# A two-layer hybrid decoder trunk: the high halves of the weights by a converting DMA, and silu through tanh

## The chip, the cores and the metric

One NeuronCore of a Trainium2 chip runs the whole program. The metric is the device time of that core in microseconds (us); lower is better.

## What is computed

Two layers, each `x + W_out[concat(mixer_g(h) * silu(z_g))]` with `h = RMSNorm(x)`, on 512 tokens of width 2048 in float32. One input projection (2048 to 7192 columns) feeds four groups of four heads. Cut to what matters:

```
h = rms_norm(x, norm_g)
p = einsum('btd,dp->btp', h, w_in)
ya = gla_mixer(aq, ak, av, alr, ...)  * silu(az)      # gated linear attention
yb = swa_mixer(bq, bk, bv, ...)       * silu(bz)      # sliding window with sinks
yc = diff_mixer(cq, ck, cv, ...)      * silu(cz)      # differential attention
yd = gdn_mixer(dqkv, dbeta, da, ...)  * silu(dz)      # gated DeltaNet
y  = concatenate([ya, yb, yc, yd]);   x = x + einsum('btm,md->btd', y, w_out)
# inside gdn_mixer:  qkv = silu(causal_conv(qkv, conv_w))
```

`silu(v) = v * sigmoid(v) = v / (1 + exp(-v))`.

## The kernel before

**Products in split precision.** Every float32 operand of a projection is split into a high half, its value rounded to `fp32r`, and a low half, the remainder. A product is three matmuls: high by high, high by low, low by high. The activations' halves (`actT_hi`, `actT_lo`) are made by ScalarE and VectorE once a layer; the weights' halves are made while they stream.

**The weight stream.** The weights lie in HBM as blocks of 128x512; one block is the weight side of one k-tile. Two blocks in a row are a pair, 128 rows of 4 KB, 512 KB. A layer has 288 k-tiles or 144 pairs, the whole program 288 pairs. SyncE (SP) brings pair `i` to `w_raw` (four buffers) once `raw_used` says that its buffer is free. GpSimd (POOL) makes from each k-tile the high half `w_hi` (line 376: add zero, write as `fp32r`) and the low half `w_lo` (line 380: `w_raw - w_hi`); both are rings of four k-tiles. It waits at line 375 for `kt_done`, so that the ring's place is free: k-tile `n` is begun when TensorE has finished k-tile `n - 4`. TensorE waits at line 407 for `w_ready`, which counts finished low halves, and then does 12 matmuls of 512 columns (line 421): three terms for each of four accumulators `acc`.

**The order of the work** is written out by hand, per engine; engines meet only through semaphores. In `project` TensorE takes a column chunk of the projection, 16 k-tiles long (12 or 4 in the output projection). Between its k-tiles it takes steps of a mixer, a generator (`gdn`, `gla`, `swa`, `dif`) whose steps are spread evenly over the chunk. A mixer's step waits in TensorE's queue for what VectorE (DVE) or ScalarE (ACT) made of the step before; while it waits, the projection behind it stands too. A layer goes through these stages:

- the chunks dq, dk, dv, dz, without a mixer (64 k-tiles). VectorE evicts dq, dk and dv (`turned_out`, line 1232) and runs the convolution and its silu over them (`conv`, lines 1252 to 1265), in the order: evict dq, convolve dq, evict dk, convolve dk, evict dv, convolve dv. TensorE cannot start the chunk after dk or dv before the accumulators are evicted
- four chunks with `gdn` for 128 tokens each, four with `gla`, two with `swa` (two token tiles each): 160 k-tiles
- four chunks of the output projection (12 k-tiles each) with `dif`, then four of 4 k-tiles each without a mixer.

**Silu.** ScalarE writes `exp(-z)` into a scratch tile (lines 916, 980, 1009, 1056, 1115). VectorE adds 1, takes the reciprocal and multiplies: lines 1260, 1263, 1265 for the 12 convolution blocks of a layer, and `gate`, lines 1197, 1199, 1201, for the 16 gates of a layer (4 mixers, 4 token tiles). In `swa` VectorE's queue reads: scores, maxima, sums for the next token tile, `gate`, the denominator, `normalise` of the next token tile (lines 1424, 1425, 1429), then the copy PT1 (line 1461) for which TensorE's product at line 660 waits. `normalise` itself waits for two inverse roots from ScalarE (line 1041; each is a Ln and an Exp with a table load ahead of both).

Of the kernel before, what the change touches and what calls it, by code (L numbers as in the profile page):

```python
# [39 lines left out]
RAW, RING = 4, 4  # L40
# [42 lines left out]
def names(fmt, *ranges):  # L83
    out = [""]
    for r in ranges:
# [25 lines left out]
    "g1 g2 g3 os redo y0 y1 y2 y3".split()  # L111


def hybrid_trunk(nc, x, wstream, wsmall, pcol, prow, wlr, cf, masks, out):
    ctx = ExitStack()
    with ctx:
# [11 lines left out]
        w_hi = sb("w_hi", [P, RING, GW], F32R)  # L128
# [105 lines left out]
        raw_used, hi_done, w_ready = sem("raw_used"), sem("hi_done"), sem("w_ready")  # L234
# [40 lines left out]
        S_DVE = Steps(sem("setup_dve"), ["ss"] + [f"rd{t}" for t in T] + ["smT", "b1", "beta", "nbeta", "av", "sp",  # L275
# [27 lines left out]
        def _(sp):  # L303
# [1308 lines left out]
```

## Time and profile before

| | us |
|---|---|
| median of 3 runs | 2127.36 (2125.7 to 2127.44) |
| the profiled execution | 2127.9 |
| its span in the trace | 2126.1 |
| TensorE busy | 2038.3 |
| GpSimd busy | 1396.3 |
| VectorE busy | 1026.4 |
| ScalarE busy | 537.6 |

The profiled execution is one run of the same program; 1.8 us of it lie outside the span. Matmuls overlap in the pipeline and their ends are modelled, so TensorE's busy time is no measure of its pace: the pace is read from how long a chain of matmuls takes, and what it loses from its waits. The granted clock is 1.00 at 2.4 GHz and 0.5 at 1.2 GHz; a stage's mean below 1.00 tells how much of it ran at the lower level.

### The profile page before, as it was taken

How to read it: one execution, taken by the hardware profiler on the slowest of the kernel's cores; microseconds unless marked ns; L12 is line 12 of the kernel's file. 1: busy time of each engine (PE TensorE's matmuls, PEld its weight loads, DVE VectorE, ACT ScalarE, POOL GpSimd, SP SyncE). 2: the span in 40 equal slices, each digit the busy share in tenths (PEclk: the TensorE clock that was granted, in tenths of full speed). 3: DMA queues.
4: the chain of work that ended last, by engine and by line, in shares of the span. 5: the costliest groups of instructions: out<-in, count | busy, mean ns of one | idle time of the engine just before them, and what ended most of it. 6: DMA issues, size and time to landing. Idle time of an engine off the chain costs nothing.

```text
span 2126.1 us, 25561 instructions
## 1 busy us (share of the span) xinstructions
PE 2038.3 (96%) x10300; PEld 1660.6 (78%) x10300; DVE 1026.4 (48%) x1407; ACT 537.6 (25%) x1014; POOL 1396.3 (66%) x1164
## 2 busy tenths in 40 slices
PE   7998999999999989999999999999999999999999
PEld 6877878878888878767888778778778787776777
DVE  1699453453222455565427984435432225545563
ACT  4010221222222443332320112221222225423220
POOL 6797654555777756557787975545557777555676
PEclk9999999999999999999999999999999999999999
DMA  5232211211222211422442322111122222132223
GB/s 216 74 96 80 70 60 50 60 60 60 80 81 88 80 60 63 146 69 80 129 132 72 99 79 63 57 60 59 51 62 87 80 80 84 55 127 81 74 85 119
DMA packets 50709, 175.92 MB, mean 83 GB/s; under 512 B 5566, under 2 KB 6304, under 8 KB 49568
## 3 DMA queue, kind: packets, MB, share of 16 engines
q1 hardware_dynamic: 44288, 155.75, 23.3%
q10 hardware_dynamic: 6304, 18.55, 2.3%
q8 instruction: 81, 1.33, 0.3%
q14 instruction: 36, 0.29, 0.0%
HBM read 165.89 MB, written 8.39 MB: 82 GB/s over the span
## 4 chain that ended last, share of the span: by engine, by line
PE 72%; DVE 20%; ACT 5%; issue 2%; DMA 1%; SPq 0%; ACTq 0%
PE acc L421 55%; DVE slots L1256 3%; DVE slots L1199 3%; DVE general L1263 3%; PE mix L488 2%; PE mix L499 1%; PE mix L682 1%; PE mix L660 1%; PE mix L528 1%; PE mix L491 1%; DVE slots L1252 1%; ACT slots L849 1%; DVE general L1319 1%; DVE slots L1429 1%; PE mix L774 1%
## 5 line engine op out<-in xcount | busy, mean ns | idle before, releaser
L376 POOL TENSOR_TENSOR w_hi<-w_raw,zeros 128x512 fp32r<-128x512 f32 x576 | 626.2, 1087 | 671.5 <-PE acc L421 648.2
L421 PE MATMUL acc<-w_hi,actT_hi 128*128 128x512 f32 x1920 | 789.0, 411 | 14.0 <-DVE slots L1232 12.1
L380 POOL TENSOR_TENSOR w_lo<-w_raw,w_hi 128x512 fp32r<-128x512 f32 x576 | 767.6, 1333 | 45.1
L421 PE MATMUL acc<-w_hi,actT_lo 128*128 128x512 f32 x1920 | 755.3, 393 | 0.0
L421 PE MATMUL acc<-w_lo,actT_hi 128*128 128x512 f32 x1920 | 753.5, 392 | 0.0
L421 PEld LDWEIGHTS acc<-w_hi,actT_hi 128*128 128x128 f32 x1920 | 364.9, 190 | 106.6 <-issue 38.7
L421 PEld LDWEIGHTS acc<-w_hi,actT_lo 128*128 128x128 f32 x1920 | 363.2, 189 | 80.3
L421 PEld LDWEIGHTS acc<-w_lo,actT_hi 128*128 128x128 f32 x1920 | 365.3, 190 | 65.5
L421 PE MATMUL acc<-actT_hi,w_hi 128*128 128x512 f32 x384 | 153.2, 399 | 2.9 <-DVE slots L1232 2.9
L421 PE MATMUL acc<-actT_hi,w_lo 128*128 128x512 f32 x384 | 150.4, 392 | 0.0
L421 PE MATMUL acc<-actT_lo,w_hi 128*128 128x512 f32 x384 | 150.4, 392 | 0.0
L849 ACT ACTIVATE slots<-acc,xr 128x512 f32<-128x512 f32 x88 | 60.2, 689 | 267.8 <-PE acc L421 267.7
L1199 DVE RECIPROCAL slots<-slots 128x512 f32<-128x512 f32 x32 | 107.3, 3353 | 1.1
L1256 DVE SCALAR_TENSOR_TENSOR slots<-slots,pcol_all 128x511 f32<-128x511 f32 (+2 forms) x72 | 99.1, 1376 | 2.6
L421 PEld LDWEIGHTS acc<-actT_hi,w_hi 128*128 128x128 f32 x384 | 72.7, 189 | 18.8 <-issue 2.2
L421 PEld LDWEIGHTS acc<-actT_hi,w_lo 128*128 128x128 f32 x384 | 72.6, 189 | 15.5
L421 PEld LDWEIGHTS acc<-actT_lo,w_hi 128*128 128x128 f32 x384 | 72.7, 189 | 15.0 <-issue 0.5
L1263 DVE RECIPROCAL general<-general 128x512 f32<-128x512 f32 x24 | 80.5, 3353 | 0.8
L916 ACT ACTIVATE general<-slots 128x512 f32<-128x512 f32 x24 | 15.2, 632 | 252.8 <-DVE slots L1256 252.8
L974 ACT ACTIVATE slots<-mix 128x512 f32<-128x512 f32 x40 | 24.0, 599 | 216.1 <-PE mix L488 216.1
L1480 DVE TENSOR_TENSOR slots<-acc,slots 128x512 f32<-128x512 f32 x64 | 42.7, 688 | 67.4 <-PE acc L421 67.4
L1376 DVE SCALAR_TENSOR_TENSOR slots<-mix,slots 128x256 f32<-128x256 f32 x8 | 3.4, 424 | 139.7 <-ACT slots L999 139.7
(250 smaller groups left out, 2095.5 us busy)
## 6 DMA issues: line engine op xcount, KB each, us to landing
w_raw<-in_wstream SPq DMA_DIRECT2D x288, 512.0 KB, 3.5
out_x<-slots ACTq DMA_DIRECT2D x7, 1024.0 KB, 4.4
slots<-in_x SPq DMA_DIRECT2D x4, 1024.0 KB, 14.5
slots<-in_x ACTq DMA_DIRECT2D x1, 4096.0 KB, 14.2
slots<-out_x ACTq DMA_DIRECT2D x1, 4096.0 KB, 15.0
out_x<-slots ACTq DMA_DIRECT2D x4, 256.0 KB, 2.3
cf_sb<-in_cf ACTq DMA_DIRECT2D x1, 964.0 KB, 11.4
slots<-in_masks ACTq DMA_DIRECT2D x1, 384.0 KB, 12.2
```

The costliest lines, as they stand in the source:

```text
L376: pool.tensor_tensor(w_hi[:, r], w_raw[:, s, k], zeros[:, :].broadcast_to([P, GW]), ALU.add) \
L380: pool.tensor_tensor(w_lo[:, r], w_raw[:, s, k], w_hi[:, r].bitcast(F32), ALU.subtract).then_inc(w_ready, 1)
L421: last = nc.tensor.matmul(acc[b][:, :], lhsT, rhs, start=(k == 0 and i == 0), stop=(k == kts - 1 and i == 2))
L488: last = nc.tensor.matmul(mh[3][:, h], U["MT"][:, h], U["X"][:, h], start=True, stop=True)
L491: last = nc.tensor.transpose(mh[1][:, h], U["X"][:, h], ident)
L499: last = nc.tensor.matmul(mh[0][:, h], U["XT"][:, h], U["Y"][:, h], start=True, stop=True)
L849: nc.scalar.activation(slot(SLOT[c])[:, b], acc[b][:, :], ACT.Copy, scale=xr[:, l, b:b + 1]) \
L974: nc.scalar.activation(U["Y"], mh[3], ACT.Copy).then_inc(*s(f"y{lv}"))
L1199: dve.reciprocal(tmp, tmp).then_inc(St.sem, St.one(f"{t}.g2"))
L1256: dve.scalar_tensor_tensor(dst[:, d:], src[:, 0:SEQ - d], tap[i], dst[:, d:], ALU.mult, ALU.add).then_inc(*ci(f"t{i}"))
L1263: dve.reciprocal(general[:, b % 2], general[:, b % 2]).then_inc(*ci("rec"))
L1480: dve.tensor_tensor(xs, acc[b][:, :], xs, ALU.add).then_inc(acc_free, 1)
```

## The change

Two parts. First, `w_hi` is no longer made by a GpSimd instruction. GpSimd issues for each pair a DMA from HBM straight into `w_hi`, now three buffers of a pair, whose type `fp32r` differs from the source's `float32`, so that the transfer converts. The source is the same `wstream` that SyncE still brings to `w_raw` (now three buffers); each weight is thus read twice. The DMA for pair `g + 1` is issued between the two low halves of pair `g`. Second, silu goes by `v * sigmoid(v) = (v/2) * (1 + tanh(v/2))`: `v` is halved where it is made (the gates' eviction scale `xr_half`, the convolution's taps), ScalarE does Tanh in place of Exp, and VectorE does one instruction in place of three.

```diff
-RAW, RING = 4, 4
+RAW, HI, RING = 3, 3, 4
...
-        w_hi = sb("w_hi", [P, RING, GW], F32R)
+        w_hi = sb("w_hi", [P, HI, 2, GW], F32R)
...
             def weights(i):
-                sp.wait_ge(raw_used, i + 1)
+                if i >= RAW:
+                    sp.wait_ge(w_ready, 2 * (i - RAW) + 2)
                 sp.dma_start(w_raw[:, i % RAW].rearrange("p a n -> p (a n)"),
...
+            def high_halves(g):
+
+                if g >= HI:
+                    pool.wait_ge(kt_done, RING + 2 * (g - HI) + 2)
+                pool.dma_start(w_hi[:, g % HI].rearrange("p a n -> p (a n)"),
+                               wstream[g:g + 1].rearrange("a p n -> p (a n)")).then_inc(hi_in[g % HI], 16)
+
+            high_halves(0)
...
-                    pool.wait_ge(raw_in[s], (l * (PAIRS // RAW) + i // RAW) * 16 + 16)
+                    pool.wait_ge(raw_in[g % RAW], g // RAW * 16 + 16)
+                    pool.wait_ge(hi_in[g % HI], g // HI * 16 + 16)
                     for k in range(2):
-                        n, r = 2 * i + k, (2 * i + k) % RING
-
-                        pool.wait_ge(kt_done, l * LAYER_KTS + (n + 1))
-                        pool.tensor_tensor(w_hi[:, r], w_raw[:, s, k], zeros[:, :].broadcast_to([P, GW]), ALU.add) \
-                            .then_inc(hi_done, 1)
-
-                        pool.wait_ge(hi_done, l * LAYER_KTS + (n + 1))
-                        pool.tensor_tensor(w_lo[:, r], w_raw[:, s, k], w_hi[:, r].bitcast(F32),
+                        n = 2 * g + k
+
+                        pool.wait_ge(kt_done, n + 1)
+                        pool.tensor_tensor(w_lo[:, n % RING], w_raw[:, g % RAW, k], w_hi[:, g % HI, k].bitcast(F32),
                                            ALU.subtract).then_inc(w_ready, 1)
-
-                    pool.wait_ge(w_ready, l * LAYER_KTS + (2 * i + 2))
-                    pool.sem_inc(raw_used, 1)
+                        if k == 0 and g + 1 < DEPTH * PAIRS:
+                            high_halves(g + 1)
...
+                    r = (xr_half if c in GATES else xr)[:, l, b:b + 1]
...
-                        nc.scalar.activation(general[:, b % 2], slot(CONV[c])[:, b], ACT.Exp, scale=-1.0) \
+                        nc.scalar.activation(general[:, b % 2], slot(CONV[c])[:, b], ACT.Tanh) \
...
+                taps = pcol_all[:, :, PC["conv"]:]
+                dve.tensor_scalar(taps, taps, 0.5, None, ALU.mult).then_inc(lam_steps, 1)
...
-                dve.tensor_scalar(tmp, tmp, 1.0, None, ALU.add).then_inc(St.sem, St.one(f"{t}.g1"))
-                dve.wait_ge(St.sem, St.at(l, f"{t}.g1"))
-                dve.reciprocal(tmp, tmp).then_inc(St.sem, St.one(f"{t}.g2"))
-                dve.wait_ge(St.sem, St.at(l, f"{t}.g2"))
-                dve.tensor_tensor(Zs, Zs, tmp, ALU.mult).then_inc(St.sem, St.one(f"{t}.g3"))
+                dve.scalar_tensor_tensor(Zs, tmp, 1.0, Zs, ALU.add, ALU.mult).then_inc(St.sem, St.one(f"{t}.g3"))
...
+                dve.tensor_scalar(xr_half[:, l], xr[:, l], 0.5, None, ALU.mult).then_inc(*si("half"))
...
-                        dve.tensor_scalar(general[:, b % 2], general[:, b % 2], 1.0, None, ALU.add) \
-                            .then_inc(*ci("one"))
-                        cw("one")
-                        dve.reciprocal(general[:, b % 2], general[:, b % 2]).then_inc(*ci("rec"))
-                        cw("rec")
-                        dve.tensor_tensor(dst, dst, general[:, b % 2], ALU.mult).then_inc(*ci("mul"))
+                        dve.scalar_tensor_tensor(dst, general[:, b % 2], 1.0, dst, ALU.add, ALU.mult) \
+                            .then_inc(*ci("mul"))
```

The four other gates' Exp become Tanh in the same way. The number of ScalarE's table loads is the same in both programs.

GpSimd's queue in the first layer's second chunk, two pairs long, before (the bracket holds the semaphores waited for; `raw_in2` is the landing of the pair's `w_raw`):

```order
L376 TENSOR_TENSOR w_hi<-w_raw,zeros 128x512 [waits kt_done,raw_in2]
L380 TENSOR_TENSOR w_lo<-w_raw,w_hi 128x512 [waits hi_done]
L376 TENSOR_TENSOR w_hi<-w_raw,zeros 128x512 [waits kt_done]
L380 TENSOR_TENSOR w_lo<-w_raw,w_hi 128x512 [waits hi_done]
L376 TENSOR_TENSOR w_hi<-w_raw,zeros 128x512 [waits w_ready,kt_done,raw_in3]
L380 TENSOR_TENSOR w_lo<-w_raw,w_hi 128x512 [waits hi_done]
L376 TENSOR_TENSOR w_hi<-w_raw,zeros 128x512 [waits kt_done]
L380 TENSOR_TENSOR w_lo<-w_raw,w_hi 128x512 [waits hi_done]
```

and the same engine and place now (`hi_in0` is the landing of the pair's converting DMA):

```order
L387 TENSOR_TENSOR w_lo<-w_raw,w_hi 128x512 [waits kt_done,hi_in0,raw_in0]
L369 DMA w_hi<-in_wstream 128x1024 [waits kt_done]
L387 TENSOR_TENSOR w_lo<-w_raw,w_hi 128x512 [waits kt_done]
L387 TENSOR_TENSOR w_lo<-w_raw,w_hi 128x512 [waits kt_done,hi_in1,raw_in1]
L369 DMA w_hi<-in_wstream 128x1024 [waits kt_done]
L387 TENSOR_TENSOR w_lo<-w_raw,w_hi 128x512 [waits kt_done]
```

The two instructions of a pair that made `w_hi` became one DMA issue, and the first `w_lo` of each pair has a new wait: the landing of a DMA that this queue issued one pair earlier.

VectorE's queue over one block of the convolution, before:

```order
L1252 TENSOR_SCALAR slots<-slots,pcol_all 128x512 [waits acc_free]
L1256 SCALAR_TENSOR_TENSOR slots<-slots,pcol_all 128x511 [waits conv_dve]
L1256 SCALAR_TENSOR_TENSOR slots<-slots,pcol_all 128x510 [waits conv_dve]
L1256 SCALAR_TENSOR_TENSOR slots<-slots,pcol_all 128x509 [waits conv_dve]
L1260 TENSOR_SCALAR general<-general 128x512 [waits conv_act]
L1263 RECIPROCAL general<-general 128x512 [waits conv_dve]
L1265 TENSOR_TENSOR slots<-slots,general 128x512 [waits conv_dve]
```

and now:

```order
L1257 TENSOR_SCALAR slots<-slots,pcol_all 128x512 [waits acc_free]
L1261 SCALAR_TENSOR_TENSOR slots<-slots,pcol_all 128x511 [waits conv_dve]
L1261 SCALAR_TENSOR_TENSOR slots<-slots,pcol_all 128x510 [waits conv_dve]
L1261 SCALAR_TENSOR_TENSOR slots<-slots,pcol_all 128x509 [waits conv_dve]
L1265 SCALAR_TENSOR_TENSOR slots<-general,slots 128x512 [waits conv_act]
```

The block ends in one instruction behind the same wait for ScalarE (`conv_act`), where it ended in three.

## Rows read from the trace of the kernel before

**Rows 1.** Waits, TensorE's own: line waited, releaser, us in total, times, longest.
```profile
PE mix L660 <- DVE slots L1461: 20.0, 6, 3.9
PE acc L421 <- DVE slots L1232: 15.0, 4, 6.1
PE mix L682 <- DVE slots L1495: 8.9, 2, 4.5
PE mix L528 <- DVE general L1352: 6.6, 8, 0.8
```

**Rows 2.** Stretches: start:end, us, busy us of PE, PEld, DVE, ACT, POOL; PEclk, DMA share, GB/s.
```profile
74.00:183.50 109.50, 101.85 (x443) 83.37 (x442) 97.39 (x79) 9.41 (x17) 86.59 (x67) 0.97 0.27 82
...
527.00:731.00 204.00, 204.00 (x1028) 163.52 (x1027) 47.72 (x75) 54.68 (x93) 148.81 (x128) 1.00 0.27 83
731.00:827.00 96.00, 85.47 (x406) 71.50 (x405) 56.91 (x76) 46.83 (x92) 55.70 (x46) 0.93 0.20 61
...
1071.00:1235.00 164.00, 156.66 (x691) 128.35 (x691) 109.88 (x99) 22.48 (x44) 132.73 (x107) 0.98 0.30 92
```

**Rows 3.** The chain of waits in order of time: start, us, 16 k-tiles of 12 matmuls.
```profile
183.52 43.66 PE acc L421 x192
```

**Rows 4.** Groups by line, VectorE, silu: count, busy us, mean ns, idle before.
```profile
L1199 DVE RECIPROCAL slots<-slots 128x512 f32<-128x512 f32 x32 | 107.3, 3353 | 1.1
...
L1263 DVE RECIPROCAL general<-general 128x512 f32<-128x512 f32 x24 | 80.5, 3353 | 0.8
...
L1201 DVE TENSOR_TENSOR slots<-slots 128x512 f32<-128x512 f32 x32 | 39.8, 1244 | 1.1
...
L1265 DVE TENSOR_TENSOR slots<-slots,general 128x512 f32<-128x512 f32 x24 | 20.2, 840 | 0.8
...
L1197 DVE TENSOR_SCALAR slots<-slots 128x512 f32<-128x512 f32 x32 | 17.1, 535 | 20.8 <-ACT slots L980 20.8
...
L1260 DVE TENSOR_SCALAR general<-general 128x512 f32<-128x512 f32 x24 | 14.0, 582 | 16.8 <-ACT general L916 16.8
```

**Rows 5.** Timeline of VectorE in `swa`, first token tile: start, us, instruction, count.
```profile
745.89 1.63 DVE L1201 TENSOR_TENSOR slots<-slots 128x512 f32<-128x512 f32 x1
...
750.59 3.19 DVE L1429 TENSOR_TENSOR slots<-slots,stat 128x512 f32<-128x512 f32 x2
753.71 0.41 DVE L1461 COPY slots<-mix 128x256 f32<-128x256 f32 x1
```

**Rows 6.** Timeline of ScalarE there: the two inverse roots' last instructions.
```profile
745.80 0.21 ACT L1041 ACTIVATE stat<-stat 128x6 f32<-128x6 f32 x1
...
748.95 0.22 ACT L1041 ACTIVATE stat<-stat 128x16 f32<-128x16 f32 x1
```

**Rows 7.** Timeline of VectorE in the third token tile of `swa`.
```profile
811.80 2.13 DVE L1429 TENSOR_TENSOR slots<-slots,stat 128x512 f32<-128x512 f32 x2
```

**Rows 8.** Timeline of ScalarE there.
```profile
810.89 0.22 ACT L1041 ACTIVATE stat<-stat 128x16 f32<-128x16 f32 x1
```

**Rows 9.** Timeline of VectorE in `dif`: four evictions behind the gate.
```profile
900.37 0.69 DVE L1201 TENSOR_TENSOR slots<-slots 128x512 f32<-128x512 f32 x1
900.98 2.48 DVE L1480 TENSOR_TENSOR slots<-acc,slots 128x512 f32<-128x512 f32 x4
```

**Rows 10.** The page's groups of GpSimd: count, busy us, mean ns, idle before.
```profile
L376 POOL TENSOR_TENSOR w_hi<-w_raw,zeros 128x512 fp32r<-128x512 f32 x576 | 626.2, 1087 | 671.5 <-PE acc L421 648.2
...
L380 POOL TENSOR_TENSOR w_lo<-w_raw,w_hi 128x512 fp32r<-128x512 f32 x576 | 767.6, 1333 | 45.1
```

**Rows 11.** The page's DMA queue of SyncE, and issues: KB each, median us to landing.
```profile
q1 hardware_dynamic: 44288, 155.75, 23.3%
...
w_raw<-in_wstream SPq DMA_DIRECT2D x288, 512.0 KB, 3.5
out_x<-slots ACTq DMA_DIRECT2D x7, 1024.0 KB, 4.4
```

**Rows 12.** Timeline of TensorE at the start.
```profile
17.75 1.09 PE L729 MATMUL mix<-cf_sb,slots 128*128 128x128 f32 x4 [3.68 <-DMA slots<-in_x]
```

More of the change, by code:

```diff
@@ L95 @@
 GDN_DVE = ("ag red qn kn qd kb ke ei es0 es1 es2 es3 mt qk xi x1 xt2 x2 xt3 x3 xt4 x4 xt5 x5 xt6 xt7 "
-           "g1 g2 g3 ub v00 v01 v02 v03 s00 s01 s02 s03 v10 v11 v12 v13 s10 s11 s12 s13 redo y0 y1 y2 y3").split()
+           "g3 ub v00 v01 v02 v03 s00 s01 s02 s03 v10 v11 v12 v13 s10 s11 s12 s13 redo y0 y1 y2 y3").split()
 GLA_PE = "u cum dec tr a us o".split()
 GLA_ACT = "abs e l eb enb er dect qkT gate sqo0 sqo1 lno ro".split()
-GLA_DVE = "g qd ki ke at0 at1 s00 s01 s10 s11 g1 g2 g3 redo y0 y1 y2 y3".split()
+GLA_DVE = "g qd ki ke at0 at1 s00 s01 s10 s11 g3 redo y0 y1 y2 y3".split()
 SWA_PE = "tr s0 s1 pt0 pt1 pv".split()
 SWA_ACT = "gate qT kT p0 p1 p2 p3 es PT0".split()
-SWA_DVE = "b0 b1 b2 b3 mx mxs nm es g1 g2 g3 den rd PT1 y0 y1 y2 y3".split()
+SWA_DVE = "b0 b1 b2 b3 mx mxs nm es g3 den rd PT1 y0 y1 y2 y3".split()
 PREP_PE = "q k".split()
@@ L150, in hybrid_trunk @@
         xr = sb("xr", [P, DEPTH, TILES])
+        xr_half = sb("xr_half", [P, DEPTH, TILES])
         def slot(n):
@@ L233, in hybrid_trunk @@
         dve_passed, pe_passed = sem("dve_passed"), sem("pe_passed")
-        raw_used, hi_done, w_ready = sem("raw_used"), sem("hi_done"), sem("w_ready")
+        hi_in = [sem(f"hi_in{i}") for i in range(HI)]
+        w_ready = sem("w_ready")
         ws_hi_done, ws_ready = sem("ws_hi_done"), sem("ws_ready")
@@ L274, in hybrid_trunk @@
                       [f"yhi{k}" for k in range(KT)])
-        S_DVE = Steps(sem("setup_dve"), ["ss"] + [f"rd{t}" for t in T] + ["smT", "b1", "beta", "nbeta", "av", "sp",
+        S_DVE = Steps(sem("setup_dve"), ["ss", "half"] + [f"rd{t}" for t in T] + ["smT", "b1", "beta", "nbeta", "av", "sp",
                                                                     "glog", "gA", "zero_gdn"] +
@@ L278, in hybrid_trunk @@
         CONV_DVE = Steps(sem("conv_dve"), [f"{c}{b}{s}" for c in ("dq", "dk", "dv") for b in range(4)
-                                           for s in ("t3", "t2", "t1", "t0", "one", "rec", "mul")])
+                                           for s in ("t3", "t2", "t1", "t0", "mul")])
         CONV_ACT = Steps(sem("conv_act"), [f"{c}{b}" for c in ("dq", "dk", "dv") for b in range(4)])
@@ L322, in _ @@
             x_in(3)
-            weights(3)
             for l in range(DEPTH):
@@ L404, in project @@
                         ahead(k)
-                    r = (kt0 + k) % RING
+                    n = l * LAYER_KTS + kt0 + k
+                    hi, lo = w_hi[:, n // 2 % HI, n % 2], w_lo[:, n % RING]
                     pe.wait_ge(w_ready, l * LAYER_KTS + (kt0 + k + 1))
@@ L414, in project @@
                         if turned:
-                            terms = [(w_hi[:, r, c], actT_hi[:, a]), (w_hi[:, r, c], actT_lo[:, a]),
-                                     (w_lo[:, r, c], actT_hi[:, a])]
-                        else:
-                            terms = [(actT_hi[:, a, c], w_hi[:, r]), (actT_hi[:, a, c], w_lo[:, r]),
-                                     (actT_lo[:, a, c], w_hi[:, r])]
+                            terms = [(hi[:, c], actT_hi[:, a]), (hi[:, c], actT_lo[:, a]), (lo[:, c], actT_hi[:, a])]
+                        else:
+                            terms = [(actT_hi[:, a, c], hi), (actT_hi[:, a, c], lo), (actT_lo[:, a, c], hi)]
                         for i, (lhsT, rhs) in enumerate(terms):
@@ L979, in _ @@
                         act.wait_ge(acc_free, acc_free_after(l, CHUNKS.index("dz"), 3))
-                    nc.scalar.activation(U["GATE"], gz, ACT.Exp, scale=-1.0).then_inc(*s("gate"))
+                    nc.scalar.activation(U["GATE"], gz, ACT.Tanh).then_inc(*s("gate"))
                     take_out(l, CHUNKS[4 + t])
@@ L1008, in _ @@
                     gz = slot(SLOT["az"])[:, t].rearrange("p (h c) -> p h c", h=HEADS)
-                    nc.scalar.activation(V["GATE"], gz, ACT.Exp, scale=-1.0).then_inc(*s("gate"))
+                    nc.scalar.activation(V["GATE"], gz, ACT.Tanh).then_inc(*s("gate"))
                     w(A_PE, "o")
@@ L1056, in _ @@
                     nc.scalar.activation(W["GATE"], slot(SLOT["bz"])[:, t].rearrange("p (h c) -> p h c", h=HEADS),
-                                         ACT.Exp, scale=-1.0).then_inc(*s("gate"))
+                                         ACT.Tanh).then_inc(*s("gate"))
                     w(B_PE, "tr")
@@ L1115, in _ @@
                     nc.scalar.activation(Z["GATE"], slot(SLOT["cz"])[:, t].rearrange("p (h c) -> p h c", h=HEADS),
-                                         ACT.Exp, scale=-1.0).then_inc(*s("gate"))
+                                         ACT.Tanh).then_inc(*s("gate"))
                     for h in H:
```

10 lines of the change are left out of this document (5 added, 5 removed).

## The prediction

> **What bounds the kernel now.** I read the waits first. TensorE waits for others in few places, and nearly all of them name VectorE [rows 1]: the output step of `swa` for the copy PT1 (20.0 us in 6 waits), the projection for the evictions of dk and dv behind the convolution (15.0 in 4), a score step of `dif` (8.9 in 2), and a state step of `gdn` (6.6 in 8). The reader is to see that GpSimd is not in this list: it makes the weight halves in time. Next the stretches [rows 2]: where those waits are long, the mean granted clock is below 1.00, so the 1.2 GHz level follows them. A clock of 0.97 over 109.5 us costs 109.5 x 0.03 = 3.3 us, 0.98 over 164.0 us another 3.3, 0.93 over 96.0 us (once in each layer) 6.7. Last the pace: 16 k-tiles in a row took 43.66 us [rows 3], 2.73 per k-tile and 5.46 per pair. 576 k-tiles make 1572 us of matmuls that this change leaves alone; the mixers' own matmuls fill most of the rest. What can be won is waits and the clock behind them; what can be lost is a weight that comes later than every 5.46 us.
>
> **Silu on VectorE.** Three instructions cost 0.54 + 3.35 + 1.24 = 5.1 us for a gate and 0.58 + 3.35 + 0.84 = 4.8 for a convolution block [rows 4]. The one that replaces them reads two SBUF tiles as L1201 and L1265 do, so I take their 0.84 to 1.24. Saved: 3.9 us for each of 32 gates, 3.5 to 4 for each of 24 blocks, some 210 us of VectorE's time. On the path only this counts:
>
> (a) Evictions of dk and dv. Four blocks stand ahead of the first and eight ahead of the second in each layer, at least 14 and 28 us sooner, where the longest wait is 6.1 [rows 1]. All 15.0 us go, and with them the slow clock, 3.3 + 3.3 [rows 2]: **21.6 us**. Next late there is TensorE itself.
>
> (b) `gdn`: 3.9 us sooner against a longest wait of 0.8 [rows 1]: **6.6 us**.
>
> (c) `swa`: here the gain is cut. VectorE's L1429 waits for ScalarE's second inverse root, which ends at 748.95 + 0.22 = 749.17; L1429 starts at 750.59 [rows 5, 6]. It can come 1.4 us sooner, not 3.9, and PT1 with it. In the third tile it starts at 811.80 and the root ends at 811.11 [rows 7, 8]: 0.7 us; the second I take as the third. Per layer 2.8, together 5.6 of the 20.0. What is late next is ScalarE with its table loads, which the change leaves. Of the 6.7 us per layer of slow clock I count a quarter: 1.7 x 2 = 3.4. Sum **9.0 us**.
>
> (d) `dif`: behind the gate stand four evictions, 2.48 us, that today start the moment the gate ends [rows 9]. With the gate 3.9 us shorter three of them (0.62 each, 1.9) can run before TensorE's chunk is over; the fourth cannot. I take 1.5 per layer, **3.0 us** of the 8.9.
>
> (e) The new halvings (twice 128x4 values, once the taps) have instructions of some 0.2 us and hide under the next transfer or chunk; Tanh takes Exp's place in the same count of instructions and table loads: 0.
>
> Sum of (a) to (e): 40.2 us.
>
> **The weights.** GpSimd loses 576 instructions of 1.09 us and keeps 576 of 1.33 [rows 10]. As it is waited for nowhere today, this gives TensorE nothing directly. VectorE shares something with it: L1201 took 1.24 us on average and the same operation in L1265 0.84 [rows 4]. Fewer such overlaps shorten steps before waits that stay; I take 2 us off, between 0 and 6.
>
> What it adds is 288 issues and a loop. The DMA of pair g+1 is issued after the first low half of pair g, and that low half waits for the landing of pair g. One turn is therefore L + 1.33 us, with L from issue to landing, and TensorE wants a pair every 5.46 us where no mixer slows it. So there is no cost up to **L = 4.1 us**. Above it the stock drains: when the issue is made on time, TensorE has four k-tiles, 10.9 us, before it needs the result, a slack of 10.9 - (L + 1.33). The pure run in each layer is dk, dv and dz, 24 pairs; `gla` goes at 204.0 / 32 = 6.38 us a pair [rows 2]. Price at L = 5.0: 2 x (24 x 0.87 - 4.6) = 33 us. At L = 5.5: 2 x (24 x 1.37 - 4.1) + 64 x 0.45 = 58 + 29 = 87 us.
>
> No row shows L for a converting DMA from GpSimd. Below: the same bytes from SyncE land in 3.5 us [rows 11]; lower would change nothing. Above: 1.09 us, the GpSimd instruction that it replaces, for the software's work, and 4.4, a transfer of twice the bytes, for running beside `w_raw`'s [rows 10, 11]: 5.5. That is no wall: a conversion that slows the movement would go beyond. I take L = 4.3, near the lower row, since it is the same transfer with an issue that is dearer, and `w_raw`'s own is issued only when the second low half is done, so they overlap little. Cost: 24 x 0.17 = 4.1 us per run, less than its slack of 5.3; I put down 1. The DMA engines hold it: `q1` moved 155.75 MB in 23.3% of the span, 314 GB/s, so a pair takes 1.7 us, two of them 3.3 of 5.46.
>
> The Trainium skill, "DMA: Bandwidth & Descriptors", section "Anatomy of one DMA — SWDGE (gpsimd) path", gives 2.0 us + bytes / 436 GB/s; for 512 KB that is 3.2 us, against the 3.5 of SyncE's row. By it the loop would take 4.5 us, the 1 us above would not be paid, and the sum would be 2087.
>
> At the start TensorE waits for the second slice of x until 17.75 us [rows 12]; the first high pair now goes among these transfers: +1.7 us.
>
> **Sum.** The profiled execution took 2127.9 (span 2126.1), 0.5 above the median of 2127.36. 2127.9 - 40.2 - 2 + 1 + 1.7 = 2088.4, as a median **2088 us**.
>
> **Rivals.**
> 1. *The loop becomes the bound.* TensorE then waits for `w_lo` in the pure chunks and, further up, in `gla`. It decides from L = 5.1, where its price reaches the 40 us. For it: a wait that did not exist, one DMA in flight at a time, unknown software and conversion. Against: 3.5 us in [rows 11], and DMA engines less than two thirds busy. At L = 5.5 the time is 2087 + 87 = 2174; at 6 it would be over 2240. Chance 0.28.
> 2. *The loop eats part*: L from 4.7 to 5.1, 2100 to 2128. Chance 0.09, a third of it within 0.2%.
> 3. *VectorE holds up the DMA's issue.* L1252 (tensor_scalar, SBUF to SBUF) runs in each convolution block and overlaps GpSimd's work, as L1201's swing above suggests for two-input ones. If one in five of the 64 pairs of the first chunks lost some 1.2 us (the 1.24 of L1201), that is 15 us: 2103. Chance 0.05. The Trainium skill, "SBUF — State Buffer", section "SBUF: two separate sides", warns of this: an fp32 VectorE operation that uses both ports keeps GpSimd from writing descriptors. No row here shows it, as no DMA starts from GpSimd.
> 4. *Only the convolution's waits go*, as every mixer step has another late partner: 2127.9 - 21.6 + 2 = 2108. Chance 0.03.
> 5. That the DMA copies and does not round would leave the time as it is forecast; it is inside the first case.
>
> **The numbers.** The forecast case has 0.55: 2068 (6 us from overlaps, and about half of what `swa` keeps of waits, 14 us, gone too) to 2100. 0.2% is 4.3 us, about what a measurement of this kernel can tell from no change. Faster by more: 0.55 + 0.05 + 0.03 + 0.04 = 0.67. Within: 0.04. Slower: 0.29. The range from 2068 to 2174 reaches to the upper bound of L and leaves out what lies beyond.
>
> **What would show it.** Right: no wait on L1237 (the evictions) in TensorE's list; PEclk 1.00 from 74 to 183 us; the wait of `swa`'s output step (line 660 before) still there, at some 14 us; the converting DMA's median landing from 3.9 to 4.5 us; no wait of TensorE for `w_lo`; k-tiles of 2.73 us in dk, dv and dz. Wrong: landings over 5 us, with TensorE waiting for GpSimd's `w_lo` and the pair pace of dv at L + 1.3. If landings are short and the time is still above 2100, then (c) or (a) failed: see which engine TensorE's waits name.

## The result, and the profile after

The changed kernel takes **2064.38 us** (median of 4 runs, 2062.99 to 2070.53) against 2126.53 for the kernel before in the same session: ratio 0.9714, 95% interval 0.9693 to 0.9735, 62 us faster. I had forecast 2088, with a range down to 2068. The direction was right, the size was not: the time lies 3.6 us below the low end.

The page of the changed kernel, busy times, the weight groups of GpSimd, and the DMA issues:

```profile
PE 2020.5 (98%) x10300; PEld 1651.3 (80%) x10300; DVE 722.4 (35%) x1298; ACT 536.4 (26%) x1014; POOL 921.9 (45%) x876
...
PE 89%; ACT 6%; DVE 3%; issue 1%; DMA 1%; SPq 0%; ACTq 0%; DVEq 0%
...
L387 POOL TENSOR_TENSOR w_lo<-w_raw,w_hi 128x512 fp32r<-128x512 f32 x576 | 756.1, 1313 | 750.4 <-DMA w_hi<-in_wstream 441.9
...
L369 POOL DMA_DIRECT2D w_hi<-in_wstream x288 | 163.6, 568 | 385.9 <-PE acc L426 377.0
...
w_hi<-in_wstream POOLq DMA_DIRECT2D x288, 512.0 KB, 3.9
w_raw<-in_wstream SPq DMA_DIRECT2D x288, 512.0 KB, 4.4
```

The second line is the chain that ended last, by engine: TensorE is 89% of it. The converting DMA lands after 3.9 us; `w_raw`, which had the DMA engines to itself before, now takes 4.4 [rows 11]. GpSimd waits 441.9 us for the high halves, and that harms nobody, as TensorE's own waits show (line waited, releaser, us in total, times, longest):

```profile
PE mix L734 <- DMA slots<-in_x: 13.9, 1, 13.9
PE mix L665 <- DVE slots L1462: 10.9, 6, 2.7
PE mix L687 <- DVE slots L1496: 7.3, 2, 3.7
PE mix L456 <- DVE slots L1304: 6.6, 6, 1.9
PE mix L477 <- ACT slots L977: 2.2, 8, 0.3
```

Against [rows 1]: the evictions (15.0) are gone, PT1 (now L665 <- L1462) fell from 20.0 to 10.9, `dif` (L687 <- L1496) from 8.9 to 7.3; the state step of `gdn` is gone; no wait names `w_lo`. L456 waits for the product ag of the next token tile of `gdn`. Before, this wait was the fourth in the list, and I used it nowhere:

```profile
PE mix L451 <- DVE slots L1303: 10.9, 6, 1.8
```

The same stretches as in [rows 2]:

```profile
74.00:183.50 109.50, 109.50 (x491) 90.62 (x490) 62.66 (x71) 10.68 (x19) 61.02 (x56) 1.00 0.61 177
527.00:731.00 204.00, 203.06 (x1026) 163.06 (x1018) 40.99 (x83) 64.98 (x113) 101.01 (x96) 1.00 0.56 165
731.00:827.00 96.00, 90.46 (x463) 76.32 (x464) 33.57 (x71) 40.69 (x82) 39.15 (x38) 0.98 0.46 137
1071.00:1235.00 164.00, 164.00 (x734) 135.30 (x733) 76.07 (x85) 16.82 (x29) 92.58 (x87) 1.00 0.61 179
```

TensorE has no gap in the first and the last of them, and the clock is 1.00 in both. VectorE's groups that answer to [rows 4]: line, shape, count, busy us, mean ns, idle before.

```profile
L1261 DVE SCALAR_TENSOR_TENSOR slots<-slots,pcol_all 128x511 f32<-128x511 f32 (+2 forms) x72 | 69.7, 968 | 2.6
L1265 DVE SCALAR_TENSOR_TENSOR slots<-general,slots 128x512 f32<-128x512 f32 x24 | 26.4, 1099 | 16.8 <-ACT general L922 16.8
L1205 DVE SCALAR_TENSOR_TENSOR slots<-slots 128x512 f32<-128x512 f32 x32 | 23.4, 732 | 20.8 <-ACT slots L986 20.8
```

The first is a surprise: the change does not touch the convolution's taps, and before they took

```profile
L1256 DVE SCALAR_TENSOR_TENSOR slots<-slots,pcol_all 128x511 f32<-128x511 f32 (+2 forms) x72 | 99.1, 1376 | 2.6
```

**Where the time came from.** I cut the traces where a k-tile's first matmul starts and sum both layers (us; a stage's length is the distance of these starts, and the last stage ends with the start of the last matmul). The columns for the two parts alone are from the first experiment. All four are profiled executions; that of the changed kernel was the longest of its four runs (2070.53), so its column shows 57.4 us less than before where the medians differ by 62.

| stage | before | silu alone | DMA alone | both (the change) | forecast gain, gain |
|---|---|---|---|---|---|
| dk, dv, dz and their evictions | 286.8 | 266.5 | 271.7 | 265.4 | 21.6, 21.4 |
| `gdn` | 595.9 | 589.5 | 578.2 | 579.2 | 6.6, 16.7 |
| `gla` | 410.4 | 410.4 | 410.4 | 410.4 | 0, 0 |
| `swa` | 259.9 | 244.4 | 240.4 | 243.1 | 9.0, 16.8 |
| output projection, `dif` | 437.6 | 436.9 | 439.7 | 436.0 | 3.0, 1.6 |
| start and both dq chunks | 131.7 | 130.7 | 130.8 | 130.7 | -1.7, 1.0 |

`gdn` carries the largest miss, 10.1 us, and `swa` the next, 7.8. The slow clock in these stages, the length of each stretch times what its granted clock lacked to 1.00, was 6.8, 0, 13.7 and 3.4 us before (first row, `gdn`, `swa`, output) and 0, 0, 5.1 and 6.8 in this profile; in `gdn` the clock has no part.

### The profile page after: what moved, and what is told of

Its sections match the earlier page's. It is cut to its first block, busy times and chain, and to the rows that moved or that the text cites. A ratio compares the mean times of both kernels' runs of the same rounds, so it can differ in the third digit from the quotient of the medians.

```text
span 2068.7 us, 24875 instructions
## 1 busy us (share of the span) xinstructions
PE 2020.5 (98%) x10300; PEld 1651.3 (80%) x10300; DVE 722.4 (35%) x1298; ACT 536.4 (26%) x1014; POOL 921.9 (45%) x876
## 4 chain that ended last, share of the span: by engine, by line
PE 89%; ACT 6%; DVE 3%; issue 1%; DMA 1%; SPq 0%; ACTq 0%; DVEq 0%
PE acc L426 70%; PE mix L493 2%; PE mix L504 1%; PE mix L687 1%; ACT L1047 1%; ACT L1044 1%; PE mix L706 1%; PE mix L496 1%; PE mix L533 1%; PE mix L665 1%; PE mix L526 1%; ACT slots L855 1%; PE mix L779 1%; PE mix L734 1%; PE mix L538 1%
## 5 line engine op out<-in xcount | busy, mean ns | idle before, releaser
L387 POOL TENSOR_TENSOR w_lo<-w_raw,w_hi 128x512 fp32r<-128x512 f32 x576 | 756.1, 1313 | 750.4 <-DMA w_hi<-in_wstream 441.9
L369 POOL DMA_DIRECT2D w_hi<-in_wstream x288 | 163.6, 568 | 385.9 <-PE acc L426 377.0
L855 ACT ACTIVATE slots<-acc,xr 128x512 f32<-128x512 f32 x56 | 38.3, 690 | 159.5 <-PE acc L426 159.4
L1261 DVE SCALAR_TENSOR_TENSOR slots<-slots,pcol_all 128x511 f32<-128x511 f32 (+2 forms) x72 | 69.7, 968 | 2.6
L1335 DVE COPY slots<-mix 128x512 f32<-128x512 f32 x40 | 27.7, 691 | 85.7 <-PE mix L496 85.7
L855 ACT ACTIVATE slots<-acc,xr_half 128x512 f32<-128x512 f32 x32 | 21.9, 689 | 125.8 <-PE acc L426 125.8
```

Of the source, the lines that this page charges most:

```text
L369: pool.dma_start(w_hi[:, g % HI].rearrange("p a n -> p (a n)"), wstream[g:g + 1].rearrange("a p n -> p (a n)")).then_inc(hi_in[g % HI], 16)
L387: pool.tensor_tensor(w_lo[:, n % RING], w_raw[:, g % RAW, k], w_hi[:, g % HI, k].bitcast(F32), ALU.subtract).then_inc(w_ready, 1)
L855: nc.scalar.activation(slot(SLOT[c])[:, b], acc[b][:, :], ACT.Copy, scale=r) \
L1261: dve.scalar_tensor_tensor(dst[:, d:], src[:, 0:SEQ - d], tap[i], dst[:, d:], ALU.mult, ALU.add).then_inc(*ci(f"t{i}"))
L1335: dve.tensor_copy(U["XT"], mh[1]).then_inc(*s(f"xt{lv}"))
```

## The experiments

**1. The two parts alone.** The silu part alone keeps this in GpSimd's loop, with the rings of before:

```diff
-                        if k == 0 and g + 1 < DEPTH * PAIRS:
-                            high_halves(g + 1)
...
+                        pool.tensor_tensor(w_hi[:, r], w_raw[:, s, k], zeros[:, :].broadcast_to([P, GW]), ALU.add) \
+                            .then_inc(hi_done, 1)
```

> The silu part of the change alone: x sigmoid(x) by the hyperbolic tangent, but GpSimd still makes the high halves with its own add, so it makes two passes of 1.1 and 1.3 us for every k-tile as before. Theory A: the changed kernel gained 10 us more in the gdn chunks than the sum had (16.7 against 6.6 us over two layers), because GpSimd lost half its passes and VectorE's operations with two SBUF operands no longer run beside them (the conv taps took 1376 ns before and 968 after, the gate product 1.24 and 0.69 us). By it this kernel lacks that part: 2126.5 - 21.6 (conv) - 6.6 (gdn) - 9 to 13 (swa) - 3 (dif) = about 2084 to 2088 us, conv taps again near 1400 ns, gdn stages of 294 us and more. Rival B: the extra gain is the silu part's own, since VectorE is free 3.4 us earlier for each gate: 2064 to 2068 us, gdn stages of 290 us, whatever the taps take.

Measured: **2082.37 us** (2079.88 to 2084.55), ratio 0.9790 [0.9777, 0.9804]. That is 1.6 us under theory A's range; its `gdn` stages (294.8 and 294.7 us) came as it said, and rival B is out. The DMA part alone keeps Exp and the three VectorE instructions:

```diff
-                dve.scalar_tensor_tensor(Zs, tmp, 1.0, Zs, ALU.add, ALU.mult).then_inc(St.sem, St.one(f"{t}.g3"))
+                dve.tensor_scalar(tmp, tmp, 1.0, None, ALU.add).then_inc(St.sem, St.one(f"{t}.g1"))
...
+                dve.reciprocal(tmp, tmp).then_inc(St.sem, St.one(f"{t}.g2"))
...
+                dve.tensor_tensor(Zs, Zs, tmp, ALU.mult).then_inc(St.sem, St.one(f"{t}.g3"))
```

> The converting DMA alone: VectorE still adds one, takes the reciprocal (3.35 us) and multiplies. Theory A (GpSimd's lost passes free VectorE): 10 to 16 us faster than before, 2111 to 2117 us; the reciprocal keeps 3.35 us, taps near 970 ns, and the wait of the conv evictions at VectorE's third block falls by a few us but stays. Rival B (the passes on GpSimd cost VectorE nothing that the end feels): 2125 to 2128 us, within 0.2% of before. If the landing time or the loop cost anything, it would be slower than 2127.

Measured: **2078.98 us** (2076.86 to 2083.05), ratio 0.9780 [0.9766, 0.9793]. Both theories for this kernel missed: theory A had the right sign and a third of the size. Alone the parts give 44.6 and 48.0 us; together 62.6. The part that I had put down at 2 us is worth as much as silu by itself (the two intervals overlap), and 30 us are claimed by both. TensorE's waits with the DMA alone:

```profile
PE mix L663 <- DVE slots L1464: 11.1, 6, 2.7
PE mix L685 <- DVE slots L1498: 8.3, 2, 4.1
PE mix L454 <- DVE slots L1306: 5.6, 6, 0.9
PE acc L424 <- DVE slots L1235: 4.1, 2, 3.5
```

The wait for PT1 is 11.1 us with all reciprocals still there, as in the changed kernel; that of the evictions fell from 15.0 to 4.1. PT1 shows why the parts don't add up: either one alone brings `normalise` up to ScalarE's second root (in the first token tile its products start 0.04 us after the root's end with the DMA alone, 0.03 us with silu alone, 1.42 us before), and neither moves the root. VectorE's groups in the same kernel show what became shorter without silu's help, and what did not move:

```profile
L1266 DVE RECIPROCAL general<-general 128x512 f32<-128x512 f32 x24 | 80.5, 3353 | 0.8
L1259 DVE SCALAR_TENSOR_TENSOR slots<-slots,pcol_all 128x511 f32<-128x511 f32 (+2 forms) x72 | 73.8, 1025 | 2.6
```

and with silu alone the taps are as slow as before:

```profile
L1258 DVE SCALAR_TENSOR_TENSOR slots<-slots,pcol_all 128x511 f32<-128x511 f32 (+2 forms) x72 | 105.1, 1459 | 2.6
```

So GpSimd's passes lengthen some of VectorE's operations and not others. The timeline of before shows one case, VectorE's rows first, then GpSimd's (start, us, instruction):

```profile
299.10 1.13 DVE L1365 SCALAR_TENSOR_TENSOR slots<-mix,stat,slots 128x128 f32<-128x128 f32 x4 [2.44 <-ACT stat L988]
300.25 1.57 DVE L1303 TENSOR_TENSOR slots<-cf_sb,glog 128x512 f32<-128x512 f32 x1
```

```profile
300.24 1.04 POOL L376 TENSOR_TENSOR w_hi<-w_raw,zeros 128x512 fp32r<-128x512 f32 x1 [0.24 <-PE acc L421]
301.36 1.60 POOL L380 TENSOR_TENSOR w_lo<-w_raw,w_hi 128x512 fp32r<-128x512 f32 x1
```

L1303 starts 0.01 us after GpSimd's add and takes 1.57 us; it reads two SBUF tiles. The add ends at 301.28, and from there L1303 runs 0.54 us. Then GpSimd's next pass takes 1.60 us in place of 1.27: each waits for the other, though some 0.15 us of each operation (0.69 against 0.54; 0.46 us of overlap against 0.33 of delay) still passes beside the other. The Trainium skill, "SBUF — State Buffer", section "SBUF: two separate sides", calls the pair of ports that the two share an exclusive lock, held by "whichever of" them "starts first", and names for VectorE its 2-port modes and operations with two SBUF inputs. These rows agree in both directions. One thing more stands in the trace of the changed kernel: L1313, also a product of two SBUF tiles, starts at 223.58 us, ahead of GpSimd's low half at 223.87, and yet takes 2.13 us. GpSimd was issuing a DMA from 223.28 to 223.84, and in all eight cases of L1313 the order is this one. So the issue itself seems to hold VectorE up as a pass does; no run tests it apart.

**2. Is it GpSimd's pass?** Put the old add back in the `gdn` stages alone, writing where the low half goes next:

```diff
                         pool.wait_ge(kt_done, n + 1)
+                        if 32 <= i < 64:
+                            pool.tensor_tensor(w_lo[:, n % RING], w_raw[:, g % RAW, k],
+                                               zeros[:, :].broadcast_to([P, GW]), ALU.add).then_inc(extra_done, 1)
+                            extras.append(n)
+                            pool.wait_ge(extra_done, len(extras))
```

> Both parts of the change, but in the 64 k-tiles of the gdn chunks (pairs 32 to 63 of each layer) GpSimd makes its old add of 1.1 us as well before each low half, into the low half's own slot, which the low half then overwrites. A k-tile takes 4.5 us there and GpSimd has time for both, so TensorE should not wait for weights. Theory A: the gdn stages of 290 us go back up by about 5 us each: 2072 to 2076 us against 2064 of the change, the gdn stage's VectorE operations with two SBUF operands 20 to 30% longer. Rival B (nothing of gdn's gain is GpSimd's doing): 2063 to 2067 us, gdn stages unchanged.

Measured: **2087.26 us** (2084.4 to 2091.83), 23 above the change; `gdn` 597.3 us for both layers against 579.2, every other stage within 4 us of the change's. In `gdn` 5.1 of the 18.1 us are slow clock, and TensorE's gaps there grew from 8.8 to 20.1 us. The direction is theory A's, the size is not: it costs more than the 8 to 12 us expected. Without the slow clock `gdn` is 2.7 us longer than with silu alone, where GpSimd makes the same two passes; what makes the difference isn't shown. A copy in its place:

```diff
-                            pool.tensor_tensor(w_lo[:, n % RING], w_raw[:, g % RAW, k],
-                                               zeros[:, :].broadcast_to([P, GW]), ALU.add).then_inc(extra_done, 1)
+                            pool.tensor_copy(w_lo[:, n % RING], w_raw[:, g % RAW, k]).then_inc(extra_done, 1)
```

> As the kernel with GpSimd's old add put back in the gdn stages (2087 us, stages of 297 and 300 us), but the extra pass is a copy with one SBUF operand in place of an add with one operand and a broadcast zero. If VectorE is held up by whatever GpSimd does in SBUF, the stages stay near 297 us in proportion to the copy's duration (2080 to 2090 us in all). If only GpSimd's two-operand operations hold it up, the stages are back at 290 us and the time at 2063 to 2068, with VectorE's products beside a copy at 0.68 us.

Measured: **2071.16 us** (2070.75 to 2071.81), 5 to 7 above the change; `gdn` 582.8. The copy lasts 617 ns where the add lasted 1064 (GpSimd's groups, the copy's kernel and the add's):

```profile
L389 POOL CAST w_lo<-w_raw 128x512 fp32r<-128x512 f32 x128 | 78.9, 617 | 135.4 <-PE acc L431 94.9
```

```profile
L389 POOL TENSOR_TENSOR w_lo<-w_raw,zeros 128x512 fp32r<-128x512 f32 x128 | 136.2, 1064 | 114.8 <-PE acc L432 80.8
```

A one-operand pass holds VectorE up too, so the second reading falls: ag takes as long beside the copy as beside the add (1290 ns; 228 to 470 us):

```profile
L1309 DVE TENSOR_TENSOR slots<-cf_sb,glog 128x512 f32<-128x512 f32 x3 | 3.9, 1289 | 0.1
```

But the price is about a quarter, not the six tenths of the first reading: the duration of the pass alone doesn't give it. Other lines differ, such as the gate's product (1338 ns against 1791); which of them makes the price isn't shown. Last, no long pass at all:

```diff
+                        c = slice(0, 8 if 32 <= i < 64 else GW)
-                        pool.tensor_tensor(w_lo[:, n % RING], w_raw[:, g % RAW, k], w_hi[:, g % HI, k].bitcast(F32),
-                                           ALU.subtract).then_inc(w_ready, 1)
+                        pool.tensor_tensor(w_lo[:, n % RING, c], w_raw[:, g % RAW, k, c],
+                                           w_hi[:, g % HI, k, c].bitcast(F32), ALU.subtract).then_inc(w_ready, 1)
```

> Both parts of the change, and in the 64 k-tiles of each gdn stage GpSimd writes only the first 8 of the 512 columns of each low half; the rest is left out. It takes the last of GpSimd's long passes away from VectorE there. Theory A (each pass holds up VectorE's operations with two SBUF operands): VectorE's products and gate operations with both operands in SBUF fall to 0.68 to 0.69 us everywhere, the gdn waits of 0.4 to 2 us a tile go, and each gdn stage falls from 289 to 290 us to 284 to 287: 2055 to 2060 us in all. Rival B (one pass in a k-tile of 4.5 us no longer stands in the path): 289 to 290 us a stage, 2062 to 2066 in all.

Measured: **2064.81 us** (2064.42 to 2068.75), no difference from the change; `gdn` 578.1. The first half of theory A holds: with GpSimd's passes gone, VectorE's operations of 228 to 470 us show their own length,

```profile
L1206 DVE SCALAR_TENSOR_TENSOR slots<-slots 128x512 f32<-128x512 f32 x3 | 2.1, 692 | 7.8 <-ACT slots L987 7.8
L1305 DVE TENSOR_TENSOR slots<-cf_sb,glog 128x512 f32<-128x512 f32 x3 | 2.1, 692 | 0.1
...
L1314 DVE TENSOR_TENSOR slots<-slots,decs 128x512 f32<-128x512 f32 x3 | 2.1, 689 | 0.0
```

where before, in the same stretch, the last two (L1303 and L1312 there) and one that reads PSUM were

```profile
L1312 DVE TENSOR_TENSOR slots<-slots,decs 128x512 f32<-128x512 f32 x4 | 6.1, 1528 | 0.0
L1303 DVE TENSOR_TENSOR slots<-cf_sb,glog 128x512 f32<-128x512 f32 x3 | 4.7, 1572 | 0.1
...
L1307 DVE TENSOR_TENSOR slots<-mix,stat 128x512 f32<-128x512 f32 x4 | 2.8, 691 | 7.7 <-ACT stat L961 7.7
```

Rival B wins on the time: the first pass that goes brings 10 us in `gdn`, the second about 1. Shorter operations that nobody waits for are worth nothing. The changed kernel shows the same from the other side: there the product L1312 (L1313 in that kernel; 183 to 470 us) takes longer than before, and `gdn` is faster all the same.

```profile
L1313 DVE TENSOR_TENSOR slots<-slots,decs 128x512 f32<-128x512 f32 x4 | 8.5, 2116 | 0.0
```

**3. How near is the loop to costing?** The issue of the high halves moves behind the second low half:

```diff
-                        if k == 0 and g + 1 < DEPTH * PAIRS:
+                        if k == 1 and g + 1 < DEPTH * PAIRS:
```

> Both parts of the change, but the DMA of the next pair's high halves is issued after the second low half of a pair, not after the first. It doubles one suspected cost, the turn of GpSimd's loop: landing 3.9 + two low halves of 1.33 = 6.6 us a pair, where it is 3.9 + 1.33 = 5.2 now and TensorE takes 5.46 us in the input's k-tiles and 6.38 in the last stage. By the prediction's formula that costs 2 x (24 x 1.1 - 4.3) + 64 x 0.2 = 44 + 13 = 57 us: 2121 us, with TensorE waiting for the low halves. Rival (transfers or the two-pair head start hide the turn): 2064 to 2070 us and no such wait. If the price is right, the loop that costs nothing now lies only about 0.3 us a pair from costing.

Measured: **2336.81 us** (2330.86 to 2340.36), ratio 1.0984 [1.0966, 1.1002]; TensorE's wait is the expected one, its price is five times the expected. TensorE's waits, GpSimd's timeline and the issues of that kernel:

```profile
PE acc L426 <- POOL w_lo L387: 183.4, 131, 4.6
```

```profile
827.34 0.57 POOL L369 DMA_DIRECT2D w_hi<-in_wstream  x1
832.48 2.52 POOL L387 TENSOR_TENSOR w_lo<-w_raw,w_hi 128x512 fp32r<-128x512 f32 x2 [4.57 <-issue]
834.95 0.57 POOL L369 DMA_DIRECT2D w_hi<-in_wstream  x1
```

```profile
w_hi<-in_wstream POOLq DMA_DIRECT2D x288, 512.0 KB, 4.9
w_raw<-in_wstream SPq DMA_DIRECT2D x288, 512.0 KB, 3.6
```

Issue to issue is 834.95 - 827.34 = 7.6 us, not 6.6. The landing grew from 3.9 to 4.9: the end of the second low half also releases SyncE's transfer, so both start together. At 7.6 the loop also passes `gla` (6.4 us a pair) and the output projection, which the formula had nearly left out: they are 66 and 63 us longer, dk, dv and dz 94. In all 37 us more than in the change are slow clock, which the formula left out too. To tell the collision from the issue itself, SyncE waits one low half longer:

```diff
-                    sp.wait_ge(w_ready, 2 * (i - RAW) + 2)
+                    sp.wait_ge(w_ready, 2 * (i - RAW) + 3)
```

> As the kernel that issues the high halves' DMA after the second low half (2336.8 us), but the raw pair's DMA on SyncE waits for one low half more. There both transfers started within 0.1 us of each other and the high halves landed after 4.87 us where it is 3.85 us in the changed kernel, so that a pair took 7.65 us and not the 6.6 of the formula. Theory A (the two transfers, of 512 KB each, share the same 16 DMA engines and the collision made the price 272 us, not 57): landing at 3.9 to 4.4 us, a turn of 6.7 to 7.1 us, and by the stages (24 input pairs above 5.46 us, 32 at 6.41, 8 at 6.1 in each layer) 2150 to 2205 us. Rival B (the landing is longer for another reason, such as GpSimd's issue following its own pass): landing 4.9 us and 2330 us or more.

Measured: **2293.67 us** (2289.45 to 2296.79), ratio 1.0781. The landing of the high halves in the first layer's dk, dv, dz fell to a median of 4.7 us (23 issues, 4.18 to 5.72), the time between issues to 7.5. That is between the theories: starting apart takes 0.2 us off the landing and 43 us off the time. That speaks for a collision, but the plain transfer now starts 1.2 to 1.6 us before the other, they still overlap by half of its length or more, and I didn't separate them fully. What else lengthens the landing, and the gap of some 0.3 us between landing and first low half, stays open.

**4. The changed kernel again.**

> The changed kernel once more, to see how far the stretches at the lower clock level vary: the profiled execution lost 12.6 us to them and its span was 2068.7 us, while the median of the timed runs was 6 us shorter. If these stretches differ from run to run, this profile shows another number of them (5 to 13 us lost) and the gdn and conv stages within 1 us of before; the median is 2063 to 2066 us.

Measured: **2065.83 us** (2063.4 to 2067.18). In this profile 7.8 us were lost to the slow clock, counted as above, in the first 12.6; the `gdn` stages were 289.1 and 289.1 us where they had been 290.1 and 289.1. So such stretches come and go after the same waits from one run to the next, and they are most of what lies between the first profiled execution (2070.53) and the median.

**5. What VectorE's order still costs.** Two waits were left that are queueing on VectorE alone. In `gdn` ag of the next tile moves ahead of this tile's gate (into a unit of its own); in `swa` PT1 moves ahead of the next tile's normalisation:

```diff
+                    if t + 1 < TILES:
+                        w(D_PE, "gap")
+                        dve.tensor_tensor(U["AG"], heads(after), cols(glog[:, t + 1]), ALU.mult) \
+                            .then_inc(D_DVE.sem, D_DVE.one(f"{t+1}.ag"))
                     gate(D_DVE, l, t, gz, U["GATE"])
...
-                    if t + 1 < TILES:
-                        normalise(t + 1)
                     w(B_PE, "pt1")
...
+                    if t + 1 < TILES:
+                        normalise(t + 1)
                     w(B_PE, "pv")
```

> Both parts of the change, and two steps of VectorE's order moved: in gdn the product ag of the next tile (own unit now, not the one of QK) is made ahead of the gate of this tile, and in swa PT1 of a tile is copied ahead of the normalisation of the next. The changed kernel's waits are 6.6 us in 6 for ag and 10.9 us in 6 for PT1. Theory: these two waits are what VectorE's order still costs, and most of both goes: 10 to 16 us, 2049 to 2055 us; what is late next in swa is the sum for the next tile's probabilities, 1 to 3 us. Rival: the copy of PT1 waits for TensorE's transposes and holds the normalisation of the next tile back, so that the scores of the next tile start later: swa stages of 61 to 64 us in place of 60.7, 2058 to 2066 us in all.

Measured: **2050.26 us** (2048.83 to 2050.76), ratio 0.9642 [0.9629, 0.9655]. The `swa` step alone:

> Both parts of the change and only the swa step moved: PT1 of a tile is copied ahead of the normalisation of the next tile. With both order changes the time was 2050.3 us and the swa stages 55.0 and 59.2 us (60.3 and 60.7 with the change alone), the gdn stages 286.8 (289.1 to 290.1). By these stages swa gives 2 x (5.3 + 1.5) = 13.6 us and gdn 5, so this kernel should take 2051 to 2056 us. Rival: the waits in swa and gdn are linked through the clock, and the swa step alone gives under 8 us (2057 and more).

Measured: **2056.6 us** (2055.32 to 2059.42), ratio 0.9672 [0.9658, 0.9687]; `swa` 228.8 us for both layers against 243.1, with no slow clock left there (5.1 before the move). It is 0.6 us past the theory's range: the moved step of `swa` gives 8 to 9 us of the 14 to 16, that of `gdn` the other 6. The stage alone gained more, 13.0 against the changed kernel's second profile (241.8); 3.4 us of it went to more slow clock in the output stages (6.8 against 3.4). Then `dif`: the sums and maxima for the first scores of the second tile go ahead of the first tile's gated products, which wait for ScalarE.

```diff
                     dve.reduce_sum(ss[:, 0:4], Z["SQO"], AX.X).then_inc(*s("redo"))
+                    if t == TILES - 1:
+                        scored(t - 1, 0)
                     w(C_ACT, "ro")
```

> The two moved steps of the kernel at 2050.3 us, and a third: in dif, VectorE adds the distances to the first scores of the second tile ahead of the gated products of the first tile, which wait 2.4 us for ScalarE's inverse root and its two table loads. TensorE waits 3.6 us there in each layer for the sum. Theory: it goes, 5 to 7 us less, 2043 to 2046 us. Rival: the wait is only put off to the next score, whose two PSUM banks are read one score later, and nothing or little is gained: 2048 to 2051 us.

Measured: **2038.85 us** (2037.61 to 2039.74), ratio **0.9587** [0.9572, 0.9601]: 11.4 us less than with two moved steps, where 5 to 7 were expected. The chunks of the second to fourth `dif` tile fell from 124.4 and 125.5 us to 119.2 and 119.1. Here the forecast left out the clock: 5.1 us of slow clock in this stage went with the wait, and 1.2 us are left in the whole profiled execution. TensorE's waits now:

```profile
PE mix L742 <- DMA slots<-in_x: 15.0, 2, 14.1
PE mix L485 <- ACT slots L985: 2.1, 8, 0.3
PE mix L673 <- ACT slots L1095: 1.1, 2, 0.6
PE mix L631 <- DVE slots L1439: 1.0, 2, 0.5
```

This version is the fastest here: 88 us under the kernel before, 25 under the change. All that is left above 2.1 us is the load of x at the start.

## Why the prediction failed

- **"I take 2 us off, between 0 and 6": the step that failed.** I wrote that GpSimd is waited for nowhere, and so its lost passes give TensorE nothing directly. Its loss was worth 2082.37 - 2064.38 = 18.0 us on top of silu (13.6 between the two profiled executions), and 48.0 alone. The rows to price it stood in the trace of before: L1201 takes 1.24 us on average where its shortest case takes 0.69, and in `gdn` L1303 stretches to 1.57 us, and TensorE waited behind both. Where L1303 (L1304 there) fell to 0.70, in the changed kernel's second token tile, the wait behind it fell from 1.82 to 0.94 us. In `gdn`, where no slow clock clouds it, the 10 us between silu alone (589.5) and the change (579.2) came with the DMA part; no wait of TensorE in either kernel names `w_lo`, and the kernel with the add put back loses them again, and more. With the DMA alone `gdn` is as short (578.2), so silu added nothing there. I had looked at silu's lines alone, and left out the 10.9 us of ag because the change doesn't touch that line.
- **(a) Evictions, 21.6: right.** 21.4 measured, no wait, clock 1.00. With silu alone it is 20.3, with the DMA alone 15.1: each part alone takes away most of the wait, and I credited one.
- **(b) `gdn`, 6.6: right for what it priced.** Silu alone gives 595.9 - 589.5 = 6.4, and the wait that I priced is gone. With the DMA alone it is gone too.
- **(c) `swa`, 9.0: 16.8 measured, the second term that was mis-sized, in the clock above all.** Of the 16.8, the slow clock is 8.6 (13.7 before, 5.1 after) and the rest 8.2; I had 3.4 and 5.6. Before, the slow clock came in six stretches of 3.4 or 6.8 us in these stages, and two are left: a quarter of it was a poor guess. The limit that I named is there: ScalarE's second root and VectorE's product, in the first tile of the changed kernel,

```profile
728.93 0.22 ACT L1047 ACTIVATE stat<-stat 128x16 f32<-128x16 f32 x1
```

```profile
729.18 2.20 DVE L1430 TENSOR_TENSOR slots<-slots,stat 128x512 f32<-128x512 f32 x2 [1.45 <-ACT stat L1047]
```

  the product starts 0.03 us after the root's end. But its two instructions took 3.19 us in [rows 5] and take 2.20 here, and the wait left over is 10.9 us, not 14.4. With silu alone it is 10.9 too, and the two take 1.81 us there although GpSimd still makes both passes: an operation that starts at another moment meets them differently, and the sum had no term for that.
- **(d) `dif`, 3.0: about right.** The wait fell by 1.6 us and the whole output projection by 1.6, in a profile with 3.4 us more of slow clock there than before; in the second profile of the changed kernel, with as much as before (3.4), it is 2.9.
- **The loop, 1 us: right.** No cost is seen. L is 3.9 us, not 4.3, and under the bound of 4.1, so no cost was due. The Trainium skill, "DMA: Bandwidth & Descriptors", section "Anatomy of one DMA — SWDGE (gpsimd) path", gives 3.2 us, 0.7 short of this transfer in company; that gives no cost either. The formula for the price was too kind: L isn't fixed (4.9 us where the turn lines the two transfers up), and beyond dk, dv, dz and `gla` it prices nothing. Rival 1's "over 2240" at L = 6 isn't what it gives either: 2087 + 2 x (24 x 1.87 - 3.6) + 64 x 0.95 = 2230.
- **The start, +1.7: 0.6 seen.** The first k-tile starts at 19.1 us, where it was 18.5; with the dq chunks the row is 1.0 us shorter even so.
- **Rival 3**, VectorE holding up the issue: no TensorE wait names `w_lo`, and of 46 landings in dk, dv and dz the longest was 4.7 us. The two engines do hold each other up, but the direction that mattered here was the other one, GpSimd holding up VectorE.

The terms of silu without the overlap, 40.2 us, stand against 44.6 measured for silu alone, the difference mostly in (c); the low end of 2068 allowed 6 us for overlaps where 18 came.

## What to carry to other kernels

An engine that nobody waits for can still set the pace: look for an operation whose mean is well over its minimum (here 1.57 against 0.69 us), see what the other engine does in those microseconds, and price the removal of that work on every stretched line that somebody waits for, not on the lines in the diff. Two edits that shorten the same queue don't add up; measure each alone. When a wait's releaser is merely late in its queue, moving one instruction ahead of work that nobody is waiting for can beat making work cheaper: three moved steps gave 25 us.

## What I had not expected of the hardware

- VectorE and GpSimd hold each other up: a 128x512 product of two SBUF tiles takes 0.69 us alone and up to 1.5 to 2.1 beside a pass. It depends on which comes first: L1310, before, starts 0.06 to 0.08 us ahead of a pass in all eight cases and takes 0.68, and it is the pass, an add of 1.04 us elsewhere, that takes 1.50. With one operand in PSUM it stays at 0.69 with GpSimd busy or not, and the reciprocal took 3352 to 3355 ns in 56 cases that all lay beside a pass. Operations with a single SBUF tile are not all safe: the taps' first product, a tensor_scalar of 128x512, took 0.47 us in the five cases without a pass beside it and 1.15 on average here, and one on 128x16 values took 1.03 with GpSimd busy throughout (before, 56 to 228 us):

```profile
L1252 DVE TENSOR_SCALAR slots<-slots,pcol_all 128x512 f32<-128x512 f32 x12 | 13.8, 1149 | 0.0
...
L1274 DVE TENSOR_SCALAR nbeta<-beta 128x16 f32<-128x16 f32 x1 | 1.0, 1029 | 0.0
```

- The converting DMA lands about as fast as a plain one (3.9 us against 3.5 for 512 KB), and its issue occupies GpSimd for 0.57 us. Where the two transfers started together, the converting one landed 1.0 us later.
